# Norm chains, 512-wide value panels and the order of the closing rows in a two-layer trunk kernel

## The reference

```python
h = modulate(rms_norm(x, norm1), sh1, sc1)
p = split_columns(h @ w_in)      # mLSTM q, k, v, o, gates; GQA q, k, v; conv u, B, C; 3 gates
merged = sigmoid(ga) * (y_m @ w_pm) + sigmoid(gb) * (y_a @ w_pa) + sigmoid(gc) * (y_c @ w_pc)
x = x + g1 * (merged @ w_o)
h2 = modulate(rms_norm(x, norm2), sh2, sc2)
x = x + g2 * (square(relu(h2 @ w_up)) @ w_down)
```

## Time and profile before

| what | value |
|---|---|
| device time, three runs | 1889.60, 1889.61, 1894.84 us (median 1889.61) |
| the profiled execution | 1894.92 us, span 1893.2 us, mean granted clock 0.988 |
| PE busy | 1851.3 us, 98% |
| PE weight loads | 1580.6 us, 83% |
| DVE / ACT / POOL busy | 1052.4 / 691.0 / 158.3 us |
| loads from memory | 242.88 MB, 129 GB/s over the span |

### The profile page before, as it was taken

The page is one execution under the profiler, slowest core; times in us unless marked ns, Lnnn a source line. Parts: engine busy times, 40 slices in busy tenths (PEclk is TensorE's granted clock), DMA queues, the critical chain, the costliest instruction groups (busy, mean ns, idle before and its releaser), DMA issues.

```text
span 1893.2 us, 25365 instructions
## 1 busy us (share of the span) xinstructions
PE 1851.3 (98%) x10461; PEld 1580.6 (83%) x10461; DVE 1052.4 (56%) x1537; ACT 691.0 (37%) x948; POOL 158.3 (8%) x158
## 2 busy tenths in 40 slices
PE   6999999999999999999999999899999999999998
PEld 4797788888888888868888888699998899989997
DVE  4535643545556665457665554643646656566555
ACT  3413543333222222333232223333644444445444
POOL 2101100001110101220000000300100110020000
PEclk8999999999999999999999999999999999999999
DMA  9221122211444453625443625232233265564653
GB/s 323 79 78 45 45 89 67 67 47 65 134 133 134 134 186 118 229 65 181 134 138 129 200 90 180 67 112 68 67 124 98 92 222 183 191 228 156 192 187 111
DMA packets 218370, 245.56 MB, mean 130 GB/s; under 512 B 5820, under 2 KB 194576, under 8 KB 218256
## 3 DMA queue, kind: packets, MB, share of 16 engines
q1 hardware_dynamic: 217952, 243.85, 40.0%
q10 hardware_dynamic: 304, 0.10, 0.0%
HBM read 242.88 MB, written 1.05 MB: 129 GB/s over the span
## 4 chain that ended last, share of the span: by engine, by line
PE 91%; DVE 4%; SPq 1%; ACT 1%; issue 1%; DMA 1%; POOL 0%; DVEq 0%; ACTq 0%; POOLq 0%
PE pp L1068 19%; PE pp L1072 19%; PE pp L1069 19%; PE pp L1077 4%; PE pp L1076 4%; PE pp L1075 4%; PE pc L1256 3%; PE pp L1050 2%; PE pp L1051 2%; PE pp L1052 2%; PE pc L1308 2%; PE pc L1346 1%; PE pc L1016 1%; PE pc L1014 1%; PE pc L1015 1%; SPq L914 1%
## 5 line engine op out<-in xcount | busy, mean ns | idle before, releaser
L1068 PE MATMUL pp<-hH,wH 128*128 128x512 f32 (+1 forms) x1760 | 589.1, 345 | 2.1 <-ACT hH L1549 2.1
L1764 DVE TENSOR_TENSOR wL<-raw,wH 128x1024 fp32r<-128x1024 f32 x358 | 449.0, 1295 | 235.4 <-ACT wH L1360 232.1
L1069 PE MATMUL pp<-hH,wL 128*128 128x512 f32 (+1 forms) x1760 | 579.1, 339 | 0.0
L1360 ACT ACTIVATE wH<-raw 128x1024 fp32r<-128x1024 f32 x360 | 360.4, 1050 | 351.6 <-PE pp L1077 135.4
L1072 PE MATMUL pp<-hL,wH 128*128 128x512 f32 (+1 forms) x1760 | 455.2, 340 | 3.0 <-POOL hL L1702 2.4
L1068 PEld LDWEIGHTS pp<-hH,wH 128*128 128x128 f32 x1760 | 333.7, 190 | 47.6 <-issue 11.6
L1069 PEld LDWEIGHTS pp<-hH,wL 128*128 128x128 f32 x1760 | 333.9, 190 | 37.5 <-issue 1.7
L1072 PEld LDWEIGHTS pp<-hL,wH 128*128 128x128 f32 x1760 | 303.0, 190 | 44.3 <-POOL hL L1702 7.3
L1068 PE MATMUL pp<-yH,wH 128*128 128x512 f32 (+1 forms) x320 | 115.3, 367 | 0.0
L1075 PE MATMUL pp<-yH,wH 128*128 128x512 f32 (+1 forms) x320 | 114.3, 357 | 0.0
L1077 PE MATMUL pp<-yH,wL 128*128 128x512 f32 (+1 forms) x320 | 114.3, 357 | 0.0
(11 more groups left out here) (249 smaller groups left out, 2250.0 us busy)
## 6 DMA issues: line engine op xcount, KB each, us to landing
raw<-in_w_in SPq DMA_DIRECT2D x84, 1024.0 KB, 5.2
raw<-in_w_up SPq DMA_DIRECT2D x32, 1024.0 KB, 5.5
raw<-in_w_down SPq DMA_DIRECT2D x32, 1024.0 KB, 5.0
pair_W<-in_w_ada SPq DMA_DIRECT2D x10, 2048.0 KB, 8.0
ada_Y<-in_w_ada SPq DMA_DIRECT2D x10, 1024.0 KB, 11.9
...
```

What stands on the lines that cost most here:

```text
L1068: pe.matmul(dsts[b], wh[b], hi[:, kt, ts_], start=first, stop=False)
L1069: pe.matmul(dsts[b], wl[b], hi[:, kt, ts_], start=False, stop=False)
L1360: act.activation(wH[:, p % HIGH, a:a + KH, :], raw[:, p % RAW, a:a + KH, :], ACT.Copy).then_inc(wH_ready, 1)
L1764: dve.tensor_tensor(wL[:, p % RAW, ks, :], raw[:, p % RAW, ks, :], wH[:, p % HIGH, ks, :].bitcast(F32), ALU.subtract).then_inc(wL_ready, 1)
```

## The change

**Norm chains.** `squares` c - 1 stands ahead of residual panel c in PLAN. Before `mean`, TensorE runs matmuls of constants (`KEEP` = 2 where all tokens are normed, 1 where only the latent are; 128x128 by 128x256, float32, into the unused half of the bank). The two `head` parts become one step, `heads`: for each row block, the 8 high matmuls of both panels and then the 4 low ones.

**Value panels.** A panel is 512 rows by 512 columns; two of them make one 512-column result, which takes both `pp` slots. 4 tiles by 4 row blocks by 3 = 48 matmuls of 512 columns a panel. DVE copies it in two parts: the first two token tiles when these have ended (`mv_half`), the others at the panel's end.

**Closing rows.** The first column half keeps its `tail` steps; the second is one step, `tail_end`, in another order, with the scale and final_norm of its half in one operation. DVE frees the slots of natural down panels without waiting for their end, TensorE doesn't wait for them, and `run_sums` waits once for each half panel.

The diff, cut to its core:

```diff
@@ -249,8 +250,7 @@
-        for c in range(2):
-            head("mk" if n == 1 else "up", l, c)
+        step("heads", l, kind="mk" if n == 1 else "up", b=0)
@@ -380,9 +380,9 @@
         for c in range(NC):
-            panel("wo", l, c)
             if c:
                 step("squares", l, n=2, j=c - 1)
+            panel("wo", l, c)
         settle()
@@ -404,12 +404,14 @@
             for c in range(NC):
-                panel("down", l, c, g)
                 if more and g == FF // D - 1 and c:
                     step("squares", l + 1, n=1, j=c - 1)
-                if not more and g == FF // D - 1 and c % 2:
+                panel("down", l, c, g)
+                if not more and g == FF // D - 1 and c == 1:
                     for tt in range(LAT // P):
-                        step("tail", l, ch=c // 2, tt=tt)
+                        step("tail", l, tt=tt)
+                if not more and g == FF // D - 1 and c == 3:
+                    step("tail_end", l)
         if more:
@@ -431,6 +433,11 @@
             st["p"], q["begun"] = q["p"], st["kts"][1]
+        elif st["k"] == "heads":
+            st["two"] = [next(q for q in plan[i:] if q["k"] == "panel" and q["c"] == c and
+                              all(q[n] == st[n] for n in ("kind", "l", "b"))) for c in range(2)]
+            for q in st["two"]:
+                q["begun"] = KH
@@ -770,16 +780,21 @@
+        def halved(st):
+            return natural(st) or st["kind"] == "mv"
         def wide(t):
...
             kind, l, c, b = st["kind"], st["l"], st["c"], st["b"]
-            if natural(st):
+            if halved(st):
                 ch, kh = divmod(c, 2)
-                rows_ = w_down[l][b * D + kh * (D // 2):b * D + (kh + 1) * (D // 2), :]
-                return rows_.rearrange("(k p) n -> p k n", p=P)[:, :, ch * (D // 2):(ch + 1) * (D // 2)]
+                w, at_ = (w_down[l][b * D:(b + 1) * D, :], 0) if kind == "down" else (w_in[l], COL["mv"])
+                return w[kh * (D // 2):(kh + 1) * (D // 2), :].rearrange("(k p) n -> p k n", p=P)[
+                    :, :, at_ + ch * (D // 2):at_ + (ch + 1) * (D // 2)]
             if kind in COL:
@@ -1004,12 +1019,13 @@
                 banks = [claim(u[tt]) if first else pc[:, u[tt][0], :] for tt in range(LAT // P)]
-                for n, (k_, tt) in enumerate(order):
+                seen = 0
+                for k_, tt in order:
                     kt = kh * KH + k_
-                    if n in (0, len(order) // 2) or end and n == KH // 2:
-                        pe.wait_ge(wL_ready, 2 * p - 1 + k_ // (KH // 2))
-                    if n == 0 or not end and tt == 0:
-                        pe.wait_ge(y_ready, y_no[l, "up", b_, (kh * KH + KH - 1 if end else kt) // 2] + 1)
+                    if k_ // (KH // 2) >= seen:
+                        pe.wait_ge(wL_ready, 2 * p - 1 + seen)
+                        pe.wait_ge(y_ready, y_no[l, "up", b_, kt // 2] + 1)
+                        seen += 1
                     ts_ = slice(CTX + tt * P, CTX + (tt + 1) * P)
@@ -1019,16 +1035,58 @@
+            def run_heads(two):
+                for st in two:
+                    pe.wait_ge(slot_free[st["p"] % 2], st["p"] // 2)
+                    pe.wait_ge(wL_ready, 2 * st["p"] - 1)
+                hi, lo, ready, need = operand(two[0])
+                ts_ = slice(0, TOK) if two[0]["kind"] == "mk" else cols(two[0]["l"])
+                each = [(pp[:, st["p"] % 2, b, ts_], st["p"] % HIGH, st["p"] % RAW, slice(b * P, (b + 1) * P))
+                        for st in two for b in range(NB)]
+                for kt in range(KH):
+                    pe.wait_ge(high_of[ready], need(kt))
+                    for dst, hs_, ls_, bs in each:
+                        pe.matmul(dst, wH[:, hs_, kt, bs], hi[:, kt, ts_], start=kt == 0, stop=False)
+                        pe.matmul(dst, wL[:, ls_, kt, bs], hi[:, kt, ts_], start=False, stop=False)
+                    pe.wait_ge(ready, need(kt))
+                    for dst, hs_, ls_, bs in each:
+                        pe.matmul(dst, wH[:, hs_, kt, bs], lo[:, kt, ts_], start=False, stop=False)
+            def run_values(st):
+                p, l, kh = st["p"], st["l"], st["c"] % 2
+                wh, wl = wide(wH[:, p % HIGH, :, :]), wide(wL[:, p % RAW, :, :])
+                pe.wait_ge(h_ready, h_no[l, 1] + KT)
+                for tt in range(TT):
+                    slot = (p - kh + tt // 2) % 2
+                    if kh == 0 and tt % 2 == 0:
+                        pe.wait_ge(slot_free[slot], (p + tt // 2) // 2)
+                    dst, ts_ = pp[:, slot, tt % 2, :], slice(tt * P, (tt + 1) * P)
+                    for k_ in range(KH):
+                        kt = kh * KH + k_
+                        if tt == 0 and k_ % 2 == 0:
+                            pe.wait_ge(wL_ready, 2 * p - 1 + k_ // 2)
+                        first, end = kt == 0, kt == KT - 1
+                        pe.matmul(dst, hH[:, kt, ts_], wh[:, k_, :], start=first, stop=False)
+                        pe.matmul(dst, hH[:, kt, ts_], wl[:, k_, :], start=False, stop=False)
+                        last = pe.matmul(dst, hL[:, kt, ts_], wh[:, k_, :], start=False, stop=end)
+                    if kh and tt == 1:
+                        last.then_inc(mv_half, 1)
+                last.then_inc(panel_done, 1)
             def run_panel(st, kts=slice(0, KT)):
...
                 slot = p % 2
+                if natural(st):
+                    run_sums(st)
+                    return
+                if kind == "mv":
+                    run_values(st)
+                    return
                 if p >= 2 and kts.start == 0:
...
                 hs_, ls_ = p % HIGH, p % RAW
-                if natural(st):
-                    run_sums(st)
-                    return
@@ -1113,6 +1173,9 @@
                         pe.wait_ge(s_const, 4)
+                    else:
+                        for i in range(KEEP if norm_cols(st).start == 0 else KEEP - 1):
+                            pe.matmul(b[:, LAT:2 * LAT], ident, ropeC, start=True, stop=True)
                     pe.wait_ge(nsum_ready, n_norm)
@@ -1245,7 +1308,7 @@
                     pe.wait_ge(mask_ready, n)
-                    pe.wait_ge(mv_ready, MH * l + h + 1)
+                    pe.wait_ge(mv_ready, MH * l + h // 2 * 2 + 2)
                     pe.wait_ge(vones, l + 1)
@@ -1502,25 +1565,38 @@
-                    ch, tt = st["ch"], st["tt"]
-                    n = 2 * ch + tt
-                    act.wait_ge(ft_ready, 2 * n + 2)
-                    if n:
+                    tt = st["tt"]
+                    act.wait_ge(ft_ready, 2 * tt + 2)
+                    if tt:
+                        act.wait_ge(fs_ready, tt)
+                    act.activation(f_sq[:, :], x_nat[:, tt, 0:D // 2], ACT.Square, accum_out=f_ss[:, tt:tt + 1]).then_inc(fs_ready, 1)
+                    act.wait_ge(fs_ready, tt + 1)
+                    act.activation(f_b[:, tt:tt + 1], f_ss[:, tt:tt + 1], ACT.Identity, scale=1.0 / D, bias=eps).then_inc(fb_ready, 1)
+                elif k == "tail_end":
+                    def square(n, tt, a, e):
+                        act.wait_ge(ft_ready, 2 * n + 2)
                         act.wait_ge(fs_ready, n)
-                    act.activation(f_sq[:, :], x_nat[:, tt, ch * (D // 2):(ch + 1) * (D // 2)], ACT.Square,
-                                   accum_out=f_ss[:, n:n + 1]).then_inc(fs_ready, 1)
-                    act.wait_ge(fs_ready, n + 1)
-                    if ch == 0:
-                        act.activation(f_b[:, tt:tt + 1], f_ss[:, n:n + 1], ACT.Identity, scale=1.0 / D,
-                                       bias=eps).then_inc(fb_ready, 1)
-                    else:
-                        act.wait_ge(fb_ready, tt + 1)
-                        act.activation(n_sd[:, tt:tt + 1], f_ss[:, n:n + 1], ACT.Sqrt, scale=1.0 / D,
-                                       bias=f_b[:, tt:tt + 1]).then_inc(fd_ready, 1)
+                        act.activation(f_sq[:, 0:e - a], x_nat[:, tt, a:e], ACT.Square, accum_out=f_ss[:, n:n + 1]).then_inc(fs_ready, 1)
+                        act.wait_ge(fs_ready, n + 1)
+                    def deviation(n, tt, i):
+                        act.wait_ge(fb_ready, i + 1)
+                        act.activation(n_sd[:, tt:tt + 1], f_ss[:, n:n + 1], ACT.Sqrt, scale=1.0 / D, bias=f_b[:, i:i + 1]
+                                       ).then_inc(fd_ready, 1)
+                    def scale_half(tt):
                         act.wait_ge(fr_ready, tt + 1)
...
                                        scale=n_rs[:, tt:tt + 1]).then_inc(fa_ready, 1)
+                    square(2, 0, D // 2, D)
+                    deviation(2, 0, 0)
+                    scale_half(0)
+                    square(3, 1, D // 2, D)
+                    deviation(3, 1, 1)
+                    scale_half(1)
                 elif k == "qss":
@@ -1813,12 +1889,23 @@
```

(70 more changed lines are left out.)

14 lines of the change are left out of this document (10 added, 4 removed).

## The result

The changed kernel takes 1874.58 us (median of 5, 1865.05 to 1876.38) against 1890.04 for the kernel before beside it (median of 5, 1889.60 to 1894.84): ratio 0.990, 95% interval [0.9873, 0.9927]. That is 15.5 us less, where 18.0 were forecast; the time lies in the range of the prediction. The profiled execution took 1876.12 us with a span of 1874.4, 18.8 us under that of before, where the sum said 20.8.

A forecast was written before the change was run, and what follows sets the result against it. TensorE, busy 98% of the span, was taken to bound the kernel. Terms of 5.1 + 2.9 + 0.85 + 4.4 + 2.0 = 15.3 us, plus 2.7 for the clock, took the 1889.6 us median to 1871.6; range 1864.5 to 1877.5.

The forecast's parts named there:

- Value panels: Value panels: 48 matmuls of 512 columns at 0.2267 us save 0.64 us a panel, 5.1 us over eight.
- Squares: Norm chains: squares one panel earlier save 2.9 us in the two all-token norms and 0.85 us in the latent-only norm.
- The price of 1 us that was kept for late splits: Latent-only part: ACT squares before splitting, so splits might delay residuals; nothing counted, 1 us kept for the range.
- Interleaved halves: Half panels behind the norms: interleaving removes waits for hL, 2.0 us layer 0, 1.3 layer 1, 1.1 latent-only.
- Rival 3: Half panels gain only a third and the closing stores collide: 1875.5 us; chance 0.08.
- Closing rows: Kernel's close: no slot wait before the last panel and earlier tails save 2.0 us; colliding stores might return 1.9 us.
- The clock: All-token norms: constant matmuls end two clock falls, 2.6 and 2.9 us, 5.5 together; counted at half, 2.7 us.
- the prediction's own last sign: Whole kernel: the prediction is wrong if the clock falls at new places; no size given.
- rival 2: Clock term is zero, or a fall arises elsewhere at some 2.9 us: 1874.3 to 1877.2 us; chance 0.15.
- The cause that stood behind the step: Norm waits: the clock falls because TensorE stands, and constant matmuls end the falls, 5.5 us for both.
- The reading of 5.3 us between the runs of before: Kernel before: the gap between runs at 1894.9 and 1889.6 us is the price of the two norm falls.
- Rival 1: All terms hold, run difference isn't norm falls: 1868.8 us; without gate column falls, to 1863; chance 0.22.

The follow-up runs named there:

- e2: The kernel before with only the squares moved one panel earlier, no constant matmuls: 1885.05 us, ratio 0.9961.
- quiet kernel: The changed kernel with gate columns spread, gate selections apart and four constant matmuls in the last attention's wait: 1867.62 us, ratio 0.9874.
- e9: The changed kernel again with no edit, five runs on one chip: median 1874.76 us, ratio 0.991 against the kernel before.
- e3: The kernel before with only the constant matmuls added, in the norms' long waits: 1889.95 us, ratio 0.9985.
- e11: The quiet kernel without the norms' constant matmuls (KEEP = 0): 1869.16 us, ratio 0.9884 against the kernel before.
- e5: The changed kernel without the constant matmuls (KEEP = 0): 1874.62 us, ratio 0.9914 against the kernel before.
- e6: The changed kernel with the two half panels behind each norm one after the other: 1878.67 us, ratio 0.9931 against the kernel before.
- e7: The changed kernel with the 32 gate column matmuls in four lots between row tiles of a value panel: 1868.04 us, ratio 0.9876.
- run 0: The text given contains no run of this name, so no change or time can be stated.

## Why the prediction was nearly right, point by point

- **Value panels, 5.1 us.** Right: 1.27 us a pair, four pairs, 5.1. The matmul of 512 columns takes 0.227 us from start to start (92.76, 92.98). By the formula of the Trainium skill (TensorE: Matmul & The Clock Gate, "Back-to-back issue gap"), given there for a matmul by itself, the eight panels would gain an estimate of 0.96 us (the prediction has 0.9). This trace doesn't agree with it.
- **Squares, 2.9 and 0.85 us.** Right. In e2's layer 0, from the ada step to the mean: 824.15 - 820.51 = 3.64 us, where 825.62 - 820.52 = 5.10 stood, 1.46 less. Latent-only, the mean of the kernel after starts 2.40 us behind the ada step, where it was 3.25: 0.85. The price of 1 us that was kept for late splits is nothing: DVE still idles 0.29 us before the last residual.
- **Interleaved halves, 4.4 us.** Right in all: 4.46 by the medians of the quiet kernel (the shares by layer were 1.94, 1.76 and 0.96, not 2.0, 1.3 and 1.1). Rival 3, a third of it, is out.
- **Closing rows, 2.0 us.** Right: 1.60 behind the last matmul and 0.43 ahead of it. No collision of the stores.
- **The clock, 5.5 us counted at half, 2.7.** This is the step that missed. In the profiled execution the two norm falls cost what was said: from the ada step to the first half's first matmul layer 0 gained 4.12 us (forecast 1.45 + 2.6) and layer 1 4.37 (1.45 + 2.9). But two falls of 1.51 us came behind the gate selections, 3.0 of the 5.5 us given back. In turn the fall in layer 1's gate columns was a short one (1274 to 1279, before 1286 to 1293): from the first value matmul to the fourth read-out layer 1 gained 3.90 us and layer 0 2.35, where the pairs account for 2.54 each, so 1.2 us more. 20.8 - 3.0 + 1.2 = 19.0 us, and the profiled executions differ by 18.8. By the prediction's own last sign, a clock that falls at new places, this step was wrong. It did little harm to the total because it had been counted at half. The terms without the clock measure 5.1 + 2.9 + 0.85 + 4.46 + 2.03 = 15.3 us; the medians moved by 15.5 in the first set and 17.2 in e9's. So the clock gave the median run 0 to 2 us, not 2.7, and less than the intervals of some 5 us can tell from either. That is rival 2, a fall arising elsewhere, which had 0.15: the median, 1874.6, lies in its 1874.3 to 1877.2 and just outside the forecast's own 1869.5 to 1874.
- **The cause that stood behind the step** was wrong in part. "The constants end the falls" failed in e3; the shorter wait took the fall away in 3 of 6 norms, and with the constants it was gone in 14 of 14 (the table above; in e11 that is one fall of 1.5 us). The reading of 5.3 us between the runs of before as these two falls is not shown: e9's runs of one program on one chip lie as far apart, with the norms at full clock in its profile. The rule of the Trainium skill (same page, "The HAM clock gate"), that equal programs can differ since the chip watches on its own, agrees with e9: 5.2 us.
- **Rival 1** (falls vanish at the gate columns) didn't occur: 0.50 at 129.0, as before.

What stays open: why the clock fell behind the gate selections of layer 0 in both profiles of the kernel after (in layer 1 in one) and in none of the kernel before, e5, e6 and e7, though TensorE's work ahead of 80 us is the same; and how often each place falls over many runs, since only profiled ones show places and fourteen are few.
